# Ten mixing groups in a 512-column form, their high parts against high and low activations in one instruction; low parts of more units on GpSimd; setup and tail reordered

## The reference, cut to what matters

```
h = rms_norm(x, mix_norm_g[i]); proj = h @ w_in[i]
da_q, da_k, da_v, s_z, s_xbc, s_dt, xa_q, gates = split_cols(proj, IN_SIZES)
xbc = silu(conv5(xbc) + conv_b)
x = x + merged @ w_out[i];  x = x + (silu(gate) * up) @ w_ffn_out[i]
```

## Time and profile before

| | |
|---|---|
| three runs | 1413.80, 1413.91, 1414.85 us |
| profiled execution | 1414.03 us, of which the profile's span is 1412.3 us |
| granted TensorE clock | 0.998 of full |
| PE busy | 1393.9 us, 99% |
| DVE, ACT, GpSimd busy | 918.5, 885.6, 322.3 us |
| HBM read | 250.18 MB |

### The profile page before, as it was taken

The page is one execution under the profiler, slowest core; times in us unless marked ns, Lnnn a source line. Parts: engine busy times, 40 slices in busy tenths (PEclk is TensorE's granted clock), DMA queues, the critical chain, the costliest instruction groups (busy, mean ns, idle before and its releaser), DMA issues.

```text
span 1412.3 us, 22092 instructions
## 1 busy us (share of the span) xinstructions
PE 1393.9 (99%) x8215; PEld 1222.1 (87%) x8231; DVE 918.5 (65%) x1243; ACT 885.6 (63%) x1432; POOL 322.3 (23%) x161
## 2 busy tenths in 40 slices
PE   7999999999999999999999999999999999999998
PEld 7899898888888889888899998988888888888886
DVE  5468575897998445554454775768889874555532
ACT  6576667986756446556445765778777464565543
POOL 0410000011023444444414000001110244344442
PEclk9999999999999999999999999999999999999999
DMA  7655445567665555666555555455756555566663
GB/s 250 189 172 174 124 134 166 159 199 200 203 194 178 183 177 180 192 192 218 185 184 170 165 152 147 133 174 143 223 190 230 179 166 192 164 194 182 192 194 119
DMA packets 157893, 252.80 MB, mean 179 GB/s; under 512 B 12649, under 2 KB 59355, under 8 KB 157787
## 3 DMA queue, kind: packets, MB, share of 16 engines
q1 hardware_dynamic: 156624, 249.50, 57.7%
q10 hardware_dynamic: 1163, 1.89, 0.4%
HBM read 250.18 MB, written 1.18 MB: 178 GB/s over the span
## 4 chain that ended last, share of the span: by engine, by line
PE 88%; DVE 4%; ACT 3%; DVEq 2%; DMA 1%; issue 1%; ACTq 0%; SPq 0%
PE PS L617 70%; PE S L617 14%; DVE wL L1367 1%; ACT wH L974 1%; PE S L624 1%; ACT scr L1135 1%; DVEq L1706 1%; DVE actLf L1635 1%; DMA w_raw<-in_w_in_dram 1%; DMA regA<-in_mem_dram 0%; PE S L936 0%; PE S L871 0%; DVEq L1637 0%; PE S L842 0%; DVE regA L1707 0%
## 5 line engine op out<-in xcount | busy, mean ns | idle before, releaser
L974 ACT CAST wH<-w_raw 128x1024 fp32r<-128x1024 f32 x440 | 457.6, 1043 | 457.4 <-PE PS L617 318.9
L1367 DVE TENSOR_TENSOR wL<-w_raw,wH 128x1024 fp32r<-128x1024 f32 (+1 forms) x328 | 416.0, 1273 | 341.9 <-ACT wH L974 323.3
L1302 POOL TENSOR_TENSOR wL<-w_raw,wH 128x1024 fp32r<-128x1024 f32 (+1 forms) x112 | 270.1, 2411 | 416.1 <-ACT wH L974 416.1
L617 PE MATMUL PS<-hHL,wH 128*128 128x256 f32 (+2 forms) x2016 | 314.8, 303 | 0.0
L617 PEld LDWEIGHTS PS<-hHL,wH 128*128 128x128 f32 (+1 forms) x2016 | 266.4, 190 | 10.9 <-issue 2.7
L617 PE MATMUL PS<-wH,actH 128*128 128x512 f32 x560 | 223.5, 399 | 0.0
L617 PE MATMUL PS<-wH,actL 128*128 128x512 f32 x560 | 218.4, 390 | 0.0
L617 PE MATMUL PS<-wH,hHL 128*128 128x512 f32 x768 | 200.7, 403 | 0.0
L617 PE MATMUL PS<-hHL,wL 128*128 128x256 f32 (+1 forms) x1168 | 172.0, 282 | 0.0
L617 PEld LDWEIGHTS PS<-wH,hHL 128*128 128x128 f32 x768 | 140.1, 188 | 33.3 <-issue 6.5
L617 PEld LDWEIGHTS PS<-hHL,wL 128*128 128x128 f32 (+1 forms) x1168 | 158.4, 190 | 6.2
(11 more groups left out here) (252 smaller groups left out, 1573.9 us busy)
## 6 DMA issues: line engine op xcount, KB each, us to landing
w_raw<-in_w_in_dram SPq DMA_DIRECT2D x192, 512.0 KB
w_raw<-in_w_ffn_in_dram SPq DMA_DIRECT2D x176, 256.0 KB
w_raw<-in_w_branch_dram SPq DMA_DIRECT2D x64, 512.0 KB
w_raw<-in_w_ffn_out_dram SPq DMA_DIRECT2D x44, 512.0 KB
w_raw<-in_w_mem_kv_dram SPq DMA_DIRECT2D x32, 512.0 KB
regA<-cs_rows SPq DMA_DIRECT2D x64, 256.0 KB, 4.9
w_raw<-in_w_out_dram SPq DMA_DIRECT2D x16, 512.0 KB
regA<-in_mem_dram SPq DMA_DIRECT2D x2, 768.0 KB, 7.0
```

Of the source, the lines that this page charges most:

```text
L617: return nc.tensor.matmul(o, l, r, start=first, stop=last, skip_group_check=True)
L974: nc.scalar.copy(wH[:, slot].rearrange("p k c -> p (k c)")[:, q], raw[:, slot].rearrange("p k c -> p (k c)")[:, q]).then_inc(h_done[slot], 1)
L1302: nc.gpsimd.tensor_tensor(wL[:, slot].rearrange("p k c -> p (k c)")[:, q], raw[:, slot].rearrange("p k c -> p (k c)")[:, q], wH[:, slot].r ...
L1367: v.tensor_tensor(wL[:, slot].rearrange("p k c -> p (k c)")[:, q], raw[:, slot].rearrange("p k c -> p (k c)")[:, q], wH[:, slot].rearrange ...
```

## The change

1. **Wide groups.** xbc4, xq0, xbc5, xq1, xbc0, q0, k0, xbc1, q1 and k1 get layout "W": a unit is four K tiles by 256 columns; two units fill a PSUM tile, so that such a group makes two fills, and a tile is needed again four units after its fill began. A unit has 8 matmuls of 512 columns (wH against hHL) and 8 of 256. The load's rows are 256 columns long instead of 512.
2. **Their evacuation.** Per fill, ACT copies the correction half (wide_corr) and DVE adds it to the main half (wide_sum), both at two steps after the fill's first unit; for xbc, ACT makes the middle tap from cin one step later (conv_mid). The copies and the xbc evacuation of ACT for these groups are gone; the conv steps stay where they are.
3. **GpSimd** also makes the low parts of the odd units 27 to 45.
4. **Setup.** The memory is loaded in four parts between the first loads; mem_turn 2 and 3 move into units 1 and 2; the fourth load goes ahead of the parameters, which now are on SP's queue; ACT's table is loaded early; par_turn and params move from units 1, 2 to 4, 5. DVE keeps the turned memory (keep), SP stores it, and layer 2 reads it back turned: its 16 transposes and statistics are gone.
5. **Ends.** The last evacuation of w_out goes ahead of that step's low part on DVE; the last two units of "down" do the first 128 tokens of both before the rest.

```diff
+    return [(kind, b, n, "W" if (kind, b) in WIDE else layout) for kind, b, n, layout in g]
+WIDE = [("xbc", 4), ("xq", 0), ("xbc", 5), ("xq", 1), ("xbc", 0), ("q", 0), ("k", 0), ("xbc", 1), ("q", 1), ("k", 1)]
+FILLS = [2 if x[3] == "W" else 1 for x in GROUPS]
+FIRST_FILL = [sum(FILLS[:i]) for i in range(NGROUPS)]
...
+        if (kind, b) in WIDE:
+            for half in range(2):
+                n = 2 * WIDE.index((kind, b)) + half
+                put(FIRST_UNIT[g] + 2 * half + 2, "act", "wide_corr", n)
+                put(FIRST_UNIT[g] + 2 * half + 2, "dve", "wide_sum", n)
+                if kind == "xbc":
+                    put(FIRST_UNIT[g] + 2 * half + 3, "act", "conv_mid", n)
...
-    mixing = FIRST_UNIT[GI["xbc", 5]] <= u < FIRST_UNIT[GI["gate1", 1]]
+    mixing = FIRST_UNIT[GI["v", 0]] <= u < FIRST_UNIT[GI["gate1", 1]]
...
             g = GI[kind, b]
-            eng.wait_ge(psum_free[g % 2], used_after(lay, g))
+            fill = FIRST_FILL[g] + FILLS[g] - 1
+            eng.wait_ge(psum_free[fill % 2], used_after(lay, fill))
...
-            load(0, 0)
-            load_mem(1)
-            for u in range(1, 3):
+            for u in range(LOOKAHEAD):
                 load(0, u)
+                load_mem(u + 1)
+            load(0, LOOKAHEAD)
...
+                if c == 0 and kind != "outb" or layout == "W" and c == 2:
+                    pe.wait_ge(psum_free[pair], lay * (LAYER_FILLS // 2) + fill // 2 + 1)
                 wait_operand(lay, kind, b, c)
                 pe.wait_ge(h_done[slot], use(lay, u) + 1)
+                if lay == 0 and kind == "mk" and b == 0 and c in (1, 2):
+                    mem_turn(c + 1)
...
+                elif layout == "W":
+                    at = 4 * (c % 2)
+                    for m in range(2):
+                        for kk in range(4):
+                            mm(dst[:, 2 * T * m:2 * T * (m + 1)], w_h[:, kk, P * m:P * (m + 1)], hHL[:, at + kk, :, :],
+                               c % 2 == 0 and kk == 0, False)
+                    pe.wait_ge(l_done[slot], use(lay, u) + 2)
+                    for m in range(2):
+                        for kk in range(4):
+                            ins = mm(dst[:, 2 * T * m:2 * T * m + T], w_l[:, kk, P * m:P * (m + 1)], hH[:, at + kk, :],
+                                     False, c % 2 == 1 and kk == 3)
...
+                if kind == "wide_corr":
+                    wait_full(act, lay, g, half)
+                    nc.scalar.copy(v3(corr[pair], 2), halves(PS[pair][:, :])[:, :, 1, :]).then_inc(wide_corr, 1)
+                elif kind == "conv_mid":
+                    act.wait_ge(wide_done, 2 * len(WIDE) * lay + i + 1)
+                    for j in range(2 * half, 2 * half + 2):
+                        ins = nc.scalar.activation(conv_tile(CONV_ORDER.index(b))[:, j, :], cin[:, j, 2:2 + T], ACT.Identity,
+                                                   bias=p_cb[:, t:t + 1], scale=p_cw[:, q:q + 1])
...
+                elif kind == "wide_sum":
+                    dve.wait_ge(wide_corr, 2 * len(WIDE) * lay + i + 1)
+                    v.tensor_tensor(dst, halves(PS[pair][:, :])[:, :, 0, :], v3(corr[pair], 2), ALU.add
+                                    ).then_inc(psum_free[pair], 1)
+                    dve.drain().then_inc(wide_done, 1)
...
-                    if i % 4 == 0:
+                    if ("xbc", b) in WIDE:
+                        dve.wait_ge(conv_mid, 8 * lay + 2 * n + i % 4 // 2 + 1)
+                    elif i % 4 == 0:
                         wait_evacuated(dve, lay, "xbc", b)
...
-            act.wait_ge(gain_ready, 1)
+            nc.scalar.activation(xsum[:, 0:1], eps, ACT.Copy, scale=eps)
+            act.wait_ge(psum_free[1], 1)
             for b in range(4):
-                mem_high(None, b, gmem[:, 0:8])
+                act.wait_ge(mem_turned, b + 1)
+                mem_high(lambda k: S[b][:, T * k:T * (k + 1)], b, gmem[:, 0:8])
                 if b < 3:
                     split_h(0, b)
             for t in range(NT):
-                mem_square(None, t)
+                mem_square(t)
...
                 def unit(u, g, c):
+                    if u == LAST_OUT:
+                        evac(lay, g)
                     split_l(lay, u + LOOKAHEAD)
```

More of the change, by code:

```diff
@@ L95 @@
 UNIT_GROUP = [i for i, x in enumerate(GROUPS) for _ in range(x[2])]
-assert UNITS % RING == 0 and NGROUPS % 2 == 0
+FILLS = [2 if x[3] == "W" else 1 for x in GROUPS]
+FIRST_FILL = [sum(FILLS[:i]) for i in range(NGROUPS)]
+LAYER_FILLS = sum(FILLS)
+PAIR = [n % 2 for n in FIRST_FILL]
+assert UNITS % RING == 0 and LAYER_FILLS % 2 == 0
 GI = {(x[0], x[1]): i for i, x in enumerate(GROUPS)}
 N_FFN = FT // 2
+LAST_OUT = FIRST_UNIT[GI["outb", 1]] + 1
 CONV_ORDER = (4, 5, 0, 1, 2, 3)
@@ L402, in build @@
         par_in, row_in, x_in, stored = (sem(n) for n in ("par_in", "row_in", "x_in", "stored"))
-        mem_in = [sem(f"mem_in{part}") for part in range(2)]
-        gain_in, gain_turned, gain_ready = (sem("mem_gain_" + n) for n in ("in", "turned", "ready"))
+        mem_in = [sem(f"mem_in{part}") for part in range(4)]
+        mem_stored = sem("mem_stored")
+        gain_in, gain_turned = sem("mem_gain_in"), sem("mem_gain_turned")
         raw_in = [sem(f"raw_in{s}") for s in range(RING)]
@@ L576, in step @@
                         sp.sem_inc(sp_pace, 1)
-                        for part in range(2):
-                            load_mem(part)
+                        sp.wait_ge(mem_stored, 16)
+                        sp.dma_start(memT, mem_rows).then_inc(mem_in[0], 16)
+                    elif kind == "mem_keep" and lay == 0:
+                        for b in range(4):
+                            sp.wait_ge(side_free[b], 2)
+                        sp.dma_start(mem_rows, keep).then_inc(mem_stored, 16)
                     elif kind == "rows":
@@ L638, in _ @@
             ins.then_inc(gain_turned, 1)
-            for b in range(4):
-                mem_turn(None, b)
-            setup_side = list(side)
+            for b in range(2):
+                mem_turn(b)
+            setup_side = [1, 1, 1, 1]
             def operand(kind):
@@ L717, in unit, with rows @@
                                      last_unit and kk == UT - 1)
-                elif kind == "down" and b == 1 and last_unit and lay == DEPTH - 1:
+                elif kind == "down" and b == 1 and c >= units - 2 and lay == DEPTH - 1:
                     pe.wait_ge(l_done[slot], use(lay, u) + 2)
-                    for t in range(NT):
+                    def rows(t, c):
+                        slot = (FIRST_UNIT[g] + c) % RING
                         for kk in range(UT):
@@ L1397, in params, with mem_factors @@
                 dve.drain()
[L1399 to L1403 removed]
+            def mem_factors():
                 for t in range(NT):
```

178 lines of the change are left out of this document (99 added, 79 removed).

## The result

The changed kernel takes 1446.82 us (median of five runs, 1445.07 to 1447.56) where the kernel before takes 1413.94: ratio 1.0232, 95% interval 1.022 to 1.0243 (so all intervals below). It is slower, by 32.9 us. The profiled executions differ by as much in span: 1445.6 against 1412.3.

A forecast was written before the change was run, and what follows sets the result against it. PE's stream of units bounds the kernel, busy 1393.9 of 1412.3 us, so every PE wait adds in full. 1414.0 + 25.0 (two layers) + 2.7 (setup) - 2.9 (the rest) = 1438.8, said as 1439; range 1417 to 1449.

The forecast's parts named there:

- the rival called the clock: Three new waits, two of 7 us and one of 5, each bring a half-rate PE stretch: 8.7 more, 1447.5; chance 0.12.
- What the wide form removes: PE's units: 2.79 us wide instead of 2.88, 40 units a layer, 3.5 us a layer, 7.0 in all saved.
- What it puts into DVE's queue, and the waits: DVE's wide_sum, 0.72 us with drain, makes PE wait: 16.0 a layer, less 3.5 is 12.5; two layers 25.0.
- the bound's terms: Waits a layer were DVE never stopped by GpSimd: put at 6.1, less 3.5 is 2.6, 5.2 in all.
- What GpSimd does to DVE: DVE operations with two SBUF inputs wait for GpSimd's low parts: DVE saves 1.15, can lose 2.4 per unit moved.
- nobody in that stretch waits for DVE: Around units 22 to 34 DVE ends step 33 6.0 us after PE begins unit 34, a lag costing nothing today.
- Setup: Before unit 3: it begins at 24.7 instead of 21.98, 2.7 us lost; bounds 1.0 and 5.
- Milder blocking: DVE gets between GpSimd's instructions or convs start earlier: layers cost 5.2 to 15, time 1419.0 to 1429; chance 0.17.
- faster: DVE's backlog goes away, step 34's sum is in time and setup gains 2 us: 1402.1; chance 0.11.
- the form not shortening: Wide units last as long as layout T units: 7.0 more, 1446; chance 0.02.

The follow-up runs named there:

- the better order: Six wide groups and norm two steps later, with mk products, parameter copies, norm root and scale one step earlier, x read before the memory's squares: 1404.44 us.

## Why the prediction was right, and what it missed

Right was the sign, the range and every place of a wait but one. The measured 1446.8 lies 7.8 us above the 1439, and within 0.7 us of the rival called the clock. That closeness is partly luck: the rival had three stretches of 2.9 us, two of them behind xa_scores(0) and one in the setup, 8.7 in all; there were five, of 1.75 us in the layers and 2.1 in the setup, 9.1 in all, and none stands behind xa_scores(0), where PE waited only 1.13.

| step (us, one layer; timeline of layer 2) | predicted | measured |
|---|---|---|
| dt_sums and unit 26 | 3.4 | 1.3 + 3.65 = 4.95 |
| unit 28 | 1.7 | 0 |
| cs_turn and unit 32 | 0.3 | 0.56 |
| unit 34 | 1.5 | 5.61 |
| xa_scores(0) | 6.9 | 1.13 |
| unit 52 | 0.6 | 0.57 |
| da_turn(3) | 1.6 | 1.6 |
| sum of waits | 16.0 | 14.4 |
| half rate behind units 26 and 34 | 0 | 3.5 |
| what the units behind waits lose besides (remainder) | 0 | 1.3 |
| wide units | -3.5 | -3.1 |
| together | 12.5 | 16.1 |
| setup, once (by unit 5) | 2.7 | 5.2 |
| layer 2's transposes, w_out, last unit, once | -2.9 | -3.5 |

Layer 1 measured 16.2. Twice the layers, with the two last rows, is 34.0; the spans differ by 33.3, and 0.6 of the difference is one unit (108 of layer 1) that lasted longer in the kernel before.

- **What the wide form removes.** Right: 0.07 to 0.09 a unit.
- **What it puts into DVE's queue, and the waits.** Right in sum within 2 us. The places shifted, both times in the same way, because GpSimd's low parts came earlier than reckoned. Those of units 35 and 37 held cs_base (2.47 us) and conv 5 (4.00), ahead of the sum that unit 34 wants, and not conv 6 behind it, so 5.61 fell on unit 34 and only 1.13 on xa_scores(0). That of unit 29 (802.78) held conv 1, ahead of unit 26's sum, and not conv 2 behind it, so unit 26 waited 3.65 and not 1.8, and unit 28 nothing where 1.7 had been put. The sums over each pair, 6.7 for 8.4 and 4.95 for 5.1 (with dt_sums), were steadier than the places. Small slips of the working change nothing: 13.1 less 11.5 is 1.6, 9.9 less 2.8 is 7.1, 40 times 0.09 is 3.6, and the bound's terms sum to 6.0.
- **What GpSimd does to DVE.** The mechanism is shown (rows of 3.92 and 4.00 for 1.83, sums at 0.69, and a mean of 481 ns for 642 once GpSimd is put back), and the rows agree with the rule of the Trainium skill that the prediction cites (GPSIMD Engine Reference, Specifications). Its weight was wrong: I wrote that were DVE never stopped, the layers would cost 5.2 in all. Taking GpSimd's share away left 24.0 of 31.8. DVE then has its own low parts to make, so that bound described a kernel that nobody can have; half rate is in the 24.0 too. And "nobody in that stretch waits for DVE" held only for a DVE as late as it was before: with GpSimd's share PE waits for it at cs_turn, and the share costs 7.6 us without any wide group.
- **Setup.** Unit 3 was put at 24.7 and came at 24.76 (the prediction's own terms sum to 16.6 + 7.9 = 24.5). Of the 2.5 us too few 2.1 are the half rate of unit 3.
- **The step that failed** is the clock: the sum puts the half rate behind its waits at nothing, and the rival that has it gets 0.12, on the ground that no row shows an array at full rate falling. The waits of the forecast itself, 3.4 to 6.9 us, were as long as the 4.0 us wait behind which the earlier trace rows show 0.21 us between matmuls. (The granted clock of the trace reads 1.00 there, from 11.50 to 14.85, so for those rows the half rate rests on the 0.21 alone; unit 3 of the changed kernel has the same 0.21 at a granted clock of 0.53.) Half-rate stretches cost 2 x 3.5 in the layers and about 2.1 in the setup, 9.1 us, and with them the forecast's own sum would have been 1448. A single estimate of waits should have carried its consequence for the clock from the start.
- **Rivals.** Milder blocking (the layers cost 32.3 us and not 5.2 to 15), faster and the form not shortening are all refuted; the faster one's condition (the sum at step 34 done 2.8 us after unit 34's start) fails by 3.0 us in the changed kernel (843.98 against 838.21 + 2.8) and costs a wait of 3.9 even with GpSimd put back.

## What to carry to other kernels

Before evacuation of PSUM moves to another engine, list for each tile who wants it next and how late the new engine is at that step, not how busy it is on average; here nearly the whole loss went with two groups of ten, and six of the others were a gain of 3.2 us. When PE has no slack, a forecast wait as long as those here (3.0 to 5.6 us) is to be priced with a half-rate stretch behind it, here of 1.4 to 2.9 us. And when one late item of a setup is pulled forward, look at what stands behind it in the same queue, since the next wait has been hidden by the first.

## What the runs showed of the hardware that I had not expected

A one-input operation of DVE was stopped as well. In the kernel with six wide groups and the norm two steps later, two scalings of x (one SBUF tile and a scalar for each partition) took 5.44 us beside two of GpSimd's low parts. In the better order they took 1.42 (GpSimd's next low part began at 35.90, 0.66 before their end), in the kernel before 2.21 (begun at 35.64, while one of GpSimd's ran until 36.64). The timelines of DVE and of GpSimd, with the norm two steps later:

```profile
40.76 5.44 DVE L1571 TENSOR_SCALAR regB<-xN,small 128x1024 f32<-128x1024 f32 x2
```

```profile
40.37 2.50 POOL L1369 TENSOR_TENSOR wL<-w_raw,wH 128x1024 fp32r<-128x1024 f32 x1 [3.22 <-ACT wH L1026]
43.08 2.57 POOL L1369 TENSOR_TENSOR wL<-w_raw,wH 128x1024 fp32r<-128x1024 f32 x1 [0.21 <-ACT wH L1026]
```

I had counted only operations with two SBUF inputs. The Trainium skill, GPSIMD Engine Reference, Specifications, names instructions in a two-port mode beside those with two SBUF inputs; the row agrees if this scaling runs in that mode, which no run here shows by itself. The other thing is that a half-rate stretch is no fixed price: it cost from 1.4 to 2.9 us behind waits between 3.0 and 5.6 us. Of waits near 2 us some were followed by one and some were not, and the length of the wait does not sort them. With all ten groups wide and GpSimd put back (two rows of PE's timeline, layer 1, units 26 and 34) the wait of 2.07 was and that of 1.86 was not:

```profile
93.22 3.47 PE L655 MATMUL PS<-hHL,wH 128*128 128x512 f32 x8 [2.07 <-DVE regA L1551]
...
120.64 2.11 PE L655 MATMUL PS<-hHL,wH 128*128 128x512 f32 x8 [1.86 <-DVE regA L1551]
```

With no wide group and GpSimd's share kept (PE's timeline, cs_turn in layers 1 and 2) it was the shorter one: behind 1.81 the granted clock fell to 0.50 from 105.20 to 106.50, behind 2.36 it stayed at 1.00 (802.20 to 805.00).

```profile
103.58 0.30 PE L955 MATMUL S<-ident,dts 128*128 128x128 f32 x1 [1.81 <-DVEq L1755]
...
802.08 0.30 PE L955 MATMUL S<-ident,dts 128*128 128x128 f32 x1 [2.36 <-DVEq L1755]
```
